# Gate projections of a hybrid decoder layer moved into the start, in quarters of the contraction, with ten slots for modulation weights

## What is computed

```python
mod = silu(c) @ w_ada + b_ada                    # 2048 x 12288
sh_m, sc_m, ga_m, sh_f, sc_f, ga_f = split(mod, 6)
h = rmsnorm(x, g_pre_mix) * (1 + sc_m) + sh_m
hq, hf, hi, hg, cq, ckv, kr, gate_a, gate_b = split(h @ w_in)
y_a = (rmsnorm(hgrn2(hq, hf, hi), g_hg_out) * silu(hg)) @ w_o_hg
y_b = attention(rmsnorm(cq), rmsnorm(ckv), kr) @ w_o_mla
merged = sigmoid(gate_a) * y_a + sigmoid(gate_b) * y_b
x = x + ga_m * rmsnorm(merged @ w_out, g_post_mix)
h = rmsnorm(x, g_pre_ffn) * (1 + sc_f) + sh_f
x = x + ga_f * rmsnorm((silu(h @ w_gate) * (h @ w_up)) @ w_down, g_post_ffn)
```

## Time and profile before

| | us |
|---|---|
| median of three runs | 1998.65 |
| profiled execution | 1998.17 |
| its span, first to last instruction | 1996.40 |
| TensorE busy, share of the span | 1849.5, 93% |
| VectorE busy | 1342.6, 67% |
| ScalarE busy | 876.6, 44% |
| GpSimd busy | 115.0, 6% |
| read from HBM | 418.55 MB |

### The profile page before, as it was taken

How to read it: one execution, slowest core, us unless ns; L and a number is a source line. 1 busy time by engine, 2 the same in 40 slices (tenths; PEclk the granted TensorE clock), 3 DMA queues, 4 the chain that set the end, 5 groups by cost and what they waited for, 6 DMA issues and landing times.

```text
span 1996.4 us, 26115 instructions
## 1 busy us (share of the span) xinstructions
PE 1849.5 (93%) x8940; PEld 1553.4 (78%) x8940; DVE 1342.6 (67%) x1486; ACT 876.6 (44%) x974; POOL 115.0 (6%) x77
## 2 busy tenths in 40 slices
PE   1548999999999999999999996999999999999996
PEld 1437888888878887888778885788888888888885
DVE  6886887787778778867777645655555555555554
ACT  4124464456446544644334443444434443444442
POOL 0000031004000400130000000000000000000000
PEclk8678999999999999999999998999999999999998
DMA  8885854784587458745778553555565556555552
GB/s 317 296 308 168 305 196 145 256 303 155 167 276 267 152 182 280 255 134 198 280 278 286 185 189 139 187 191 189 186 193 191 190 187 198 189 189 188 190 190 73
DMA packets 116225, 421.77 MB, mean 211 GB/s; under 512 B 12976, under 2 KB 13104, under 8 KB 115888
## 3 DMA queue, kind: packets, MB, share of 16 engines
q1 hardware_dynamic: 116144, 420.70, 62.8%
HBM read 418.55 MB, written 2.10 MB: 211 GB/s over the span
## 4 chain that ended last, share of the span: by engine, by line
PE 79%; DVE 9%; DMA 8%; issue 3%; ACT 1%; DVEq 0%; SPq 0%; POOL 0%; ACTq 0%; POOLq 0%
PE PS L677 24%; PE PS L679 23%; PE PS L678 23%; DMA ada_raw<-in_ada 5%; DVE ada_acc L1077 3%; PE PS L862 2%; DMA raw<-in_ada 2%; DVE ada_acc L987 2%; PE PS L686 1%; DVE wlo L973 1%; DMA raw<-in_w_c 1%; PE PS L712 1%; PE PS L807 1%; PE PS L806 1%; PE PS L933 0%
## 5 line engine op out<-in xcount | busy, mean ns | idle before, releaser
L973 DVE TENSOR_TENSOR wlo<-raw,whi 128x1024 fp32r<-128x1024 f32 (+1 forms) x600 | 734.1, 1228 | 412.7 <-ACT whi L377 412.6
L377 ACT ACTIVATE whi<-raw 128x1024 fp32r<-128x1024 f32 (+1 forms) x600 | 629.3, 1053 | 805.4 <-PE PS L679 658.9
L677 PE MATMUL PS<-whi,hT_hi 128*128 128x512 f32 x1664 | 661.4, 397 | 52.4 <-DVE hT_lo L1057 40.6
L679 PE MATMUL PS<-whi,hT_lo 128*128 128x512 f32 x1664 | 652.1, 392 | 0.0
L678 PE MATMUL PS<-wlo,hT_hi 128*128 128x512 f32 x1664 | 651.8, 392 | 0.0
L677 PEld LDWEIGHTS PS<-whi,hT_hi 128*128 128x128 f32 x1664 | 315.2, 189 | 120.8 <-DVE hT_lo L1057 41.0
L679 PEld LDWEIGHTS PS<-whi,hT_lo 128*128 128x128 f32 x1664 | 314.7, 189 | 67.3
L678 PEld LDWEIGHTS PS<-wlo,hT_hi 128*128 128x128 f32 x1664 | 315.4, 190 | 63.0
L987 DVE SCALAR_TENSOR_TENSOR ada_acc<-ada_raw,csilu,ada_acc 128x512 f32<-128x512 f32 x240 | 180.2, 751 | 68.9 <-DMA ada_raw<-in_ada 64.0
L677 PE MATMUL PS<-whi,oT_hi 128*128 128x512 f32 x480 | 187.8, 391 | 2.4 <-DVE oT_lo L1437 2.4
L679 PE MATMUL PS<-whi,oT_lo 128*128 128x512 f32 x480 | 187.5, 391 | 0.0
(11 more groups left out here) (196 smaller groups left out, 1432.7 us busy)
## 6 DMA issues: line engine op xcount, KB each, us to landing
ada_raw<-in_ada SPq DMA_DIRECT2D x128, 512.0 KB, 4.7
raw<-in_w_gate SPq DMA_DIRECT2D x88, 512.0 KB, 3.4
raw<-in_w_up SPq DMA_DIRECT2D x88, 512.0 KB, 3.3
raw<-in_w_down SPq DMA_DIRECT2D x88, 512.0 KB, 3.4
raw<-in_ada SPq DMA_DIRECT2D x64, 512.0 KB, 4.7
raw<-in_w_hf SPq DMA_DIRECT2D x32, 512.0 KB, 5.4
raw<-in_w_hq SPq DMA_DIRECT2D x32, 512.0 KB, 4.9
raw<-in_w_hi SPq DMA_DIRECT2D x32, 512.0 KB, 4.7
```

The source lines that it names most:

```text
L377: nc.scalar.activation(whi[:, pl.slot(c), 0:w], raw[:, pl.slot(c), 0:w], ACT.Copy)\
L677: nc.tensor.matmul(o, hi[:, kt, tok], whi[:, s, cols], start=start, stop=False)
L679: last = nc.tensor.matmul(o, lo[:, kt, tok], whi[:, s, cols], start=False, stop=stop)
L973: nc.vector.tensor_tensor(wlo[:, s, 0:w], raw[:, s, 0:w], whi[:, s, 0:w].bitcast(F32), ALU.subtract)\
```

## The change

1. **Gates in the start.** A quarter of the start now has ten groups of two chunks (`SG` = 10: two of `w_c`, eight of the gates) in place of two, 20 chunks in place of 4, so the start has 80 chunks and the gate stage is gone. Every group accumulates over two chunks alone. In the first quarter ScalarE copies the sums out of PSUM, in the later three VectorE adds them (`add_pair`). The sigmoids are taken on ScalarE in the last quarter, and stay in the tile `gate`.
2. **Modulation 1024 wide.** A chunk of modulation is now one row tile by 1024 columns; one instruction of 128x1024 takes the place of two of 128x512. Its loads in the start go to ten slots, which are tiles not yet in use. In a pass there are 32 chunks in place of 24, at chunks 3 to 18 and 24 to 39 of the pass, through two slots as before.
3. **Merging.** In the last 16 chunks of a pass VectorE multiplies each finished pair by its gate (into `zT`) and then adds it to `merged`: two instructions of 128x1024 where there was one.
4. **Smaller.** The transposes of the merged rows are spread over the first group of `w_out`; both gain rows are spread in the `w_out` stage, the second no longer at the very end; the masks are bytes; the mean square of x stands behind the thirteenth chunk of modulation; one clear of GpSimd goes, one is moved.

The core of the diff. Sizes and tiles first:

```diff
-ADA_A = 3
+ADA_A = 2
+ADA_W = 2 * NW
+ADA_SLOTS = 10
+ADA_STEPS = 12
+PH = 4
+SG = 2 + 2 * GD
+W_G = CD // PH
...
-ya = sb("ya", [P, TT, D])
-yb = sb("yb", [P, TT, D])
+gate = sb("gate", [P, 2, TT, D])
+merged = sb("merged", [P, TT, D])
+yb, ya = gate[:, 0], gate[:, 1]
...
+ada0_slot = [ada_raw[:, 0], ada_raw[:, 1], dec[:, 0], dec[:, 1], zT[:, 0], zT[:, 1]]
+ada0_slot += [t[:].rearrange("p i s -> p (i s)") for t in (pT, bT, qT, kT)]
...
+        def ada_due(i):
+            return -(-min(i, ADA_STEPS) * KD // ADA_STEPS)
...
-        A_ADA, G_ADA = 3, 4
+        ADA_AT = [3, 3 * CD]
```

The loads of the start, on SP:

```diff
-            for n in range(QUARTERS):
-                for c in range(0 if n else RING, ADA_Q):
...
+            def load_ada0(a):
+                if a >= ADA_SLOTS:
+                    sp.wait_ge(ada_step, a - ADA_SLOTS + 1)
+                sp.dma_start(ada0_slot[a % ADA_SLOTS], ada0[a]).then_inc(ada_loaded[a % ADA_SLOTS], 16)
+            for a in range(4):
+                load_ada0(a)
+            sp.dma_start(yb, x).then_inc(sig("x_loaded"), 16)
+            for a in range(4, KD):
+                load_ada0(a)
...
+            for c in range(RING):
+                load(start, c, w_start[c])
+            for a in range(KD, KD + ADA_SLOTS):
+                load_ada0(a)
...
+            for n in range(PH):
+                for i in range(SG * W_G):
+                    c = n * SG * W_G + i + RING
+                    if c < N_C:
+                        load(start, c, w_start[c])
+                    for a in range((n + 1) * KD + ada_due(i) + ADA_SLOTS, (n + 1) * KD + ada_due(i + 1) + ADA_SLOTS):
+                        if a < ADA0:
+                            load_ada0(a)
```

TensorE's start:

```diff
+            sum_quarter(0)
+            for n in range(PH):
                 pe.wait_ge(sig("h_low"), (n + 1) * KP_Q)
-                for j in range(2):
-                    multiply(pl, j, CD, 2 * n + 2 * j, 2 * n, 2 * n + 2, hT_hi, hT_lo)
+                for j in range(SG):
+                    multiply(pl, n * SG + j, W_G, (n * SG + j) * W_G, 0, W_G, hT_hi, hT_lo, kt0=n * W_G * KC)
+                    if j == 6 and n < PH - 1:
+                        sum_quarter(n + 1)
```

TensorE's gate stage, and below it the stage of `w_out`:

```diff
-            with pe.Fori(0, GD) as n:
-                pl = place_gate(n)
-                multiply(pl, 0, CD, 0, 0, CD, hT_hi, hT_lo)
-                multiply(pl, 1, CD, CD, 0, CD - 1, hT_hi, hT_lo)
...
+            for c in range(CD):
+                pe.wait_ge(sig("m_low"), c + 1)
+                multiply(pl, 0, CD, 0, c, c + 1, hT_hi, hT_lo)
+                if c + 4 < CD:
+                    transpose_merged(c + 4)
+            for j in range(1, GD):
+                if j <= 2:
+                    spread_gain(j)
+                multiply(pl, j, CD, j * CD, 0, CD, hT_hi, hT_lo)
```

VectorE's start:

```diff
+            for a in range(KD):
+                ada0_chunk(a)
+                if a == 3 * KD // 4:
+                    dve.wait_ge(sig("x_squared"), TT)
+                    nc.vector.tensor_scalar(stat[:, 0:TT], stat[:, 0:TT], 1.0 / D, EPS, ALU.mult, ALU.add)
...
+            for c in range(N_C + AHEAD):
+                low(pl, c)
+                n, i = divmod(c, SG * W_G)
+                for a in range((n + 1) * KD + ada_due(i), (n + 1) * KD + ada_due(i + 1)):
+                    if a < ADA0:
+                        ada0_chunk(a)
+                if i == 16 and n < PH - 1:
+                    shift_and_scale(n + 1)
+                if i == 18 and n < PH - 1:
+                    quarter_low(n + 1)
+                j, odd = divmod(c - AHEAD, W_G)
+                if odd == W_G - 1 and SG <= j:
+                    add_pair(pl, j, c - AHEAD, start_sum[j % SG])
```

VectorE in the last 16 chunks of a pass:

```diff
-                        add_pair(pl, 8 + n, c - 3, sums_of[:, :, (n % GD) * NW:(n % GD + 1) * NW])
+                        dve.wait_ge(multiplied, pl.through(c - 3))
+                        if n == 1:
+                            dve.wait_ge(sig("cross_scored"), g + 1)
+                        nc.vector.tensor_tensor(scaled[n % 2], banks(2 * p), start_sum[2 + n], ALU.mult)\
+                          .then_inc(pair_free[p], 1)
...
+                        nc.vector.tensor_tensor(cols, cols, scaled[n % 2], ALU.add).then_inc(sig("merges"), 1)
```

More of the change, by code:

```diff
@@ L24 @@
 I32 = mybir.dt.int32
+U8 = mybir.dt.uint8
 ACT = mybir.ActivationFunctionType
@@ new lines, in _, with load, load_ada @@
+            for a in range(4, KD):
+                load_ada0(a)
+            def load(pl, c, src, width=NW):
+                if not pl.starts(c):
+                    sp.wait_ge(lo_ready, pl.through(c) - RING)
+                sp.dma_start(raw[:, pl.slot(c), 0:KC * width], src).then_inc(raw_loaded[pl.slot(c)], 16)
+            def load_ada(g, a):
+                sp.wait_ge(ada_step, g * (ADA_A * KD) + (ADA0 + a - 1))
+                sp.dma_start(ada_raw[:, a % 2], ada1[g * (ADA_A * KD) + a]).then_inc(ada_loaded[a % 2], 16)
@@ L738, in _ @@
-            pe.wait_ge(sig("c_normed"), TT)
-            transpose_group(stage, XA).then_inc(sig("c_transposed"), 1)
-            pe.wait_ge(pair_free[pl.pair(2)], pl.freed(2))
-            pe.wait_ge(sig("kr_loaded"), 16)
-            for tt in range(TT):
-                for k in range(KD):
-                    o = PS[:, 2 * pl.pair(2) + tt, 0:ROPE]
-                    at = (k % 2) * T + tt * P
-                    last = nc.tensor.matmul(o, xT[:, k // 2, at:at + P], key_weights[:, k * ROPE:(k + 1) * ROPE],
-                                            start=k == 0, stop=k == KD - 1)
@@ new lines, in kr_multiply @@
+            def kr_multiply():
+                pe.wait_ge(sig("kr_loaded"), 16)
+                for tt in range(TT):
+                    for k in range(KD):
+                        o = PS[:, XB + tt, 0:ROPE]
+                        at = (k % 2) * T + tt * P
+                        last = nc.tensor.matmul(o, xT[:, k // 2, at:at + P], key_weights[:, k * ROPE:(k + 1) * ROPE],
+                                                start=k == 0, stop=k == KD - 1)
+                last.then_inc(sig("kr_multiplied"), 1)
@@ L1364, in _, with gain_pair @@
                                         ALU.subtract).then_inc(sig("m_low"), 1)
-            dve.wait_ge(sig("mods_d"), GD)
+            def gain_pair(j):
+                dve.wait_ge(multiplied, pl.through((j + 1) * CD - 1))
+                p = pl.pair(j)
+                dve.wait_ge(sig("gain_copied"), 2)
+                dve.wait_ge(sig("y_squared"), (j + 1) * TT)
+                nc.vector.tensor_tensor(ya[:, :, j * NW:(j + 1) * NW], banks(2 * p),
+                                        post_gain[0][:, j * NW:(j + 1) * NW].unsqueeze(1)
+                                        .broadcast_to([P, TT, NW]), ALU.mult)\
+                  .then_inc(pair_free[p], 1)
+            for kp in range(4):
+                merged_low(kp)
+            for c in range(AHEAD, CD):
+                low(pl, c)
+                if c < CD - 1:
+                    merged_low(c + 1)
+            make_gain(1, C_GPOST, GA_M)
             nc.vector.scalar_tensor_tensor(out=scale_h[:], in0=mods[:, SC_F:SC_F + KD], scalar=1.0,
```

541 lines of the change are left out of this document (241 added, 300 removed).

## The result

| | before | after |
|---|---|---|
| median of four runs, us | 1998.2 | 1981.9 |
| profiled execution, us | 1998.17 | 1982.95 |
| its span, us | 1996.40 | 1981.0 |
| TensorE busy, us | 1849.5 | 1859.5 |
| VectorE busy, us | 1342.6 | 1375.7 |

The ratio of the times is 0.9911, with a 95% interval of 0.9896 to 0.9925: faster, by 16 us where 40 were forecast. The stage bounds are TensorE's first instructions, as in the earlier trace rows; a pass begins with its first multiply.

A forecast was written before the change was run, and what follows sets the result against it. The prediction took TensorE to bound the passes and modulation the start. From 1998.2 us, the gate stage gave -183.6, the start +115.8, the passes +28 and the entry to `w_out` 0: 1958, with an 8-in-10 range of 1926 to 1988.

The forecast's parts named there:

- What bounds the kernel: Whole kernel: TensorE bounds the passes, modulation the start; of 174 us of gates, 58 fit into the start's waits.
- The start: Start of the kernel: first multiply at 51 us, end at 294.5 instead of 178.74, +115.8 us.
- The passes: Four passes: level 0 late by 4.4 us, later levels cost 2.6; 7 a pass, +28 us in all.
- the signs that the prediction named: First multiply at 49 to 56, passes from near 294, 196 us a pass, 4 us idle ahead of level 0's scores.
- Rival 3: Levels of the passes: GpSimd holds VectorE, 0.44 us an instruction, 19.8 a pass; 2009 us in all, chance 0.07.
- Rival 2: Start: transfers at 259 GB/s pace it, first multiply at 56, three quarters in 190 us; 1973 us, chance 0.12.
- Rival 1: Start and level 0: VectorE keeps enough in hand, nothing waits; start -10, passes -28, 1920 us; chance 0.17.
- From the gates to `w_out`: Stretch from the last multiply to `w_out`: about 9 us as before, change 0, bounds -5 and +4.

The follow-up runs named there:

- fill_wait: Changed kernel with sixteen matmuls of 128x512, result unread, on TensorE ahead of its wait for level 0's product: 1978.7 us, ratio 0.9901.
- short_diffs: Changed kernel with GpSimd's differences covering a quarter of their elements in levels 0 to 6 (values not the reference's): 1971.5 us, ratio 0.9861.
- more slots: Changed kernel with the passes' modulation loads through up to four slots and issued two chunks earlier: 1971.2 us, ratio 0.9871.
- all_short_diffs: all_three with GpSimd's differences a quarter as long in levels 0 to 6 (values not the reference's): 1929.1 us, ratio 0.9657.
- all_three: gap_slots with the mean square of x behind the sixth modulation instruction of the first quarter in place of the thirteenth: 1945.3 us, ratio 0.9730.
- gap_slots: Changed kernel with both the loads of more slots and the second modulation group placed as in gap: 1948.9 us, ratio 0.9752.
- gap: Changed kernel with a pass's second modulation group at chunks 23 to 26 and 32 to 43 in place of 24 to 39: 1968.6 us, ratio 0.9855.
- tail: all_three with the second modulation group at chunks 23, 24, 24, 25, 25, 26, 26, 33, 34, 36, 37, 39, 40, 42, 42, 43: 1926.2 us.
- late_loads: tail with the first modulation group's loads of a pass issued two chunks later: 1931.8 us, ratio 0.9662.

## Why the prediction was off

*What bounds the kernel*: right. TensorE bounds the passes, and the start hid 62 of 174 us of gate matmuls, where 58 were worked out.

*The start*: right to 3.6 us of 115.8. The first multiply was forecast at 51 and came at 50.31. The instruction of 128x1024 that no trace had shown, 1.28 us from the line through two other shapes, took 1.281. TensorE's waits for VectorE were put at 10, for `wlo`, and are 4.5 (2.9 and 1.6 us, for the sums `gate` and `side`); that is more than the whole difference. VectorE itself waits 32.6 us for `whi` there, so it had more in hand than the sum gave it.

*The passes*: +28 forecast, +54.5 measured, and this is the step that failed. Its idle time came out right, 29 us more on TensorE, but by luck, for it isn't where the step had it: 20 us stand at level 0 and just ahead of it, where 17.6 were forecast, 2 at the later levels in place of 10.4, and 7 in the first eight chunks of a pass, where the step had nothing. Along TensorE's timeline the four passes lost 6.0 us in their first eight chunks, 3.1 from there to the first attention scores, 23.0 from these to level 0, 12.1 from level 0 to level 1, 5.4 over the later levels and 5.0 behind them. Three things are missing from the step.

First, **what stands behind a wait**. The step priced each wait by its length. The trace showed a chunk at 1.2 GHz costing 2.6 us more, and the start was charged with it once; the waits that the change itself makes were not. TensorE is busy 22 us more with the same matmuls, 15 of them by the lower clock. With these 22 the sum would have been 1980. They aren't a price of the clock alone, though: in fill_wait the clock was kept up at level 0, and the passes gained 3 us, since VectorE is late at level 1 as well.

Second, the extra sums of modulation on TensorE, 32 matmuls, 3.4 us, which ran in the gate stage before and stand in the passes now.

Third, **GpSimd's hold** at level 0, and the loads. Counted from the first attention scores, level 0 is 5.7 to 5.9 us later than before in a pass, where the step had 4.4; with most of the hold away (short_diffs) it is 3.6 to 4.4. So the place was priced about right, and the hold was left out: it was given to a rival, at 0.11 us in the mean of sixteen `low`, most of which met no difference of GpSimd; the change puts modulation beside the differences, and each such instruction is held by 0.8 to 1.0. It is 10 us in the changed kernel and 16 to 21 once the loads and the place of level 0 are out of the way. The loads were counted at the levels alone; in the first eight chunks they cost TensorE the 7 us above, which go with more slots.

Of the signs that the prediction named, the first multiply, the start of the passes and the 4 us ahead of level 0 came; a pass takes 203 us in place of 196, and new idle time stands elsewhere too. VectorE's busy time is 1375.7 in place of about 1340: in the passes it is 632.5 in short_diffs where the changed kernel has 655.7, so 23 of it is the hold.

*Rival 3* had the right mechanism, with a wrong price. The Trainium skill ("SBUF — State Buffer", Who interferes with whom) has VectorE's two-input instructions and GpSimd's reads exclude each other, and the traces agree: 1.28 us becomes 2.06 to 2.29, while the product that reads PSUM keeps its 1.21. The rival's price of 15 us a pass for the levels was too high, though its 0.44 for one instruction was too low: where the hold stood alone (all_short_diffs against all_three) it was 4 to 5 a pass. And the hold is shared: 1.28 plus the 1.04 of a free difference is about what both then take.

*Rival 2* (the transfers pace the start) didn't happen: the passes begin at 291. The transfers had their share in the passes instead, where the two slots were left as they were; the sum had 0.5 us for each late load, and gap_slots against gap shows 20 us in all (16 by the passes).

*Rival 1* (nothing waits) at 1920 is nearly what the same work costs when placed otherwise: 1926 in the run named tail.

*From the gates to `w_out`*: 0 forecast, +2.9 measured up to the feed-forward part. The entry is shorter by 5.7 us (1102.55 to 1106.04 in place of 9.2), and the transposes and gain rows give 8.6 back inside the stage.

The range (1926 to 1988) held the result; the forecast of 1958 was 24 us low.

## To carry to other kernels

When a change adds a wait to the engine that bounds a stage, price the wait and then the stretch behind it, from a row at the lower clock: here 29 us of new waits came with 22 us of longer busy time. Keeping the engine at work in the wait gave only 3 us back, so remove the lateness first. Before work is moved onto an engine that "has a third of its time free", look at the few instructions of the other engine that stand in order behind it, and put the work where the chain has slack: the passes with the same modulation cost 54 us more in one order and 10 in another, with earlier loads. Test single fixes together too: gap and slots brought 13 and 11 us alone, and 33 together.

## What was not expected of the hardware

A VectorE instruction with two SBUF inputs and a GpSimd difference that overlap take turns, as the rows above fit, so that each takes up to about the sum of both lengths: GpSimd's differences in the passes went from 1771 and 1321 ns in the mean to 2029 and 1986 with no change in their code. Even an instruction of 64 columns, 0.27 us, was held for 0.8 to 0.9.

The return of a hardware loop cost TensorE 0.7 us or less where the first modulation loads of a pass were issued behind the sixth chunk of weights (the changed kernel, gap, short_diffs, late_loads), and 1.4 to 3.3 us where they were issued two chunks earlier.
